# The semaphore wait in front of the first matmul block of a channel group, in a hybrid Conformer/SSD/MoE step

## The reference

```
u = xn @ w_in                                  # 1024 -> 10272 columns
glu_v, glu_g, z, xbc, dt_raw, gate_logit = split(u)
a    = causal_dwconv(glu_v * sigmoid(glu_g))   # 31 taps
xs, bm, cm = split(silu(causal_dwconv(xbc)))   # 4 taps
y, h = ssd(xs, dt, A, bm, cm, h0)              # chunked scan, and new states
y    = group_norm((y + d_skip * xs) * silu(z))
gates = sigmoid(gate_logit + gate_b)
```

## Time and profile before

| | us |
|---|---|
| median of 3 runs (1586.05 to 1589.49) | 1589.34 |
| the profiled execution | 1590.23 |
| its span, first to last instruction | 1588.5 |
| PE / DVE / ACT / POOL busy | 1383.0 / 1151.7 / 817.7 / 209.9 |

### The profile page before, as it was taken

The page is one execution under the profiler, slowest core; times in us unless marked ns, Lnnn a source line. Parts: engine busy times, 40 slices in busy tenths (PEclk is TensorE's granted clock), DMA queues, the critical chain, the costliest instruction groups (busy, mean ns, idle before and its releaser), DMA issues. The chain is left out here.

```text
span 1588.5 us, 25995 instructions
## 1 busy us (share of the span) xinstructions
PE 1383.0 (87%) x8618; PEld 1216.4 (77%) x8618; DVE 1151.7 (72%) x1626; ACT 817.7 (51%) x1437; POOL 209.9 (13%) x328
## 2 busy tenths in 40 slices
PE   4988998989989899898994899997449999999980
PEld 4887987979879798797982799985347878787860
DVE  4457796877968779687786454542739999999964
ACT  4343463534635346353452332422138999999961
POOL 1012030120301203012030000000200111111112
PEclk9888998989989899898995999999669999999995
DMA  6141623515235162351633825310678999999936
GB/s 191 41 127 55 167 72 93 157 54 169 67 97 152 54 169 67 101 148 54 173 90 129 247 63 171 117 54 19 273 257 310 371 371 372 370 374 374 373 117 238
DMA packets 191725, 273.99 MB, mean 172 GB/s; under 512 B 15661, under 2 KB 154117, under 8 KB 175252
## 3 DMA queue, kind: packets, MB, share of 16 engines
q1 hardware_dynamic: 179100, 248.36, 47.2%
q0 software_dynamic: 9536, 17.98, 3.2%
q10 hardware_dynamic: 3040, 7.03, 1.2%
HBM read 238.21 MB, written 52.48 MB: 183 GB/s over the span
## 5 line engine op out<-in xcount | busy, mean ns | idle before, releaser
L882 PE MATMUL pu<-xh,wh 128*128 128x304 f32 (+1 forms) x1280 | 297.2, 315 | 30.2 <-ACTq L720 28.6
L882 PE MATMUL pu<-xh,wl 128*128 128x304 f32 (+1 forms) x1280 | 282.2, 303 | 0.0
L882 PE MATMUL pu<-xl,wh 128*128 128x304 f32 (+1 forms) x1280 | 282.0, 303 | 0.0
L882 PEld LDWEIGHTS pu<-xh,wh 128*128 128x128 f32 x1280 | 208.7, 201 | 55.4 <-ACTq L720 30.6
L882 PEld LDWEIGHTS pu<-xl,wh 128*128 128x128 f32 x1280 | 210.4, 201 | 0.0
L882 PEld LDWEIGHTS pu<-xh,wl 128*128 128x128 f32 x1280 | 208.9, 200 | 0.0
L526 ACT ACTIVATE wh<-ring 128x1024 fp32r<-128x1024 f32 x80 | 84.4, 1055 | 226.8 <-PE pu L882 223.3
L1023 DVE SCALAR_TENSOR_TENSOR cacc<-a_p,gc,cacc 128x528 f32<-128x528 f32 x232 | 190.6, 822 | 5.0
L1742 DVE TENSOR_TENSOR W13l<-W,W13h 128x1024 fp32r<-128x1024 f32 x160 | 185.0, 1217 | 2.6 <-issue 0.3
L1726 ACT ACTIVATE W13h<-W 128x1024 fp32r<-128x1024 f32 x160 | 156.3, 1063 | 0.2 <-issue 0.2
L237 DVE TENSOR_TENSOR wl<-ring,wh 128x1024 fp32r<-128x1024 f32 x80 | 101.1, 1264 | 54.4 <-ACT wh L526 51.0
(11 more groups left out here) (396 smaller groups left out, 2633.6 us busy)
## 6 DMA issues: line engine op xcount, KB each, us to landing
W<-in_exp_w SPq DMA_DIRECT2D x100, 1024.0 KB, 7.4
ring<-in_w_in SPq DMA_DIRECT2D x80, 512.0 KB, 4.1
x<-in_exp_w SPq DMA_DIRECT2D x20, 1024.0 KB, 7.8
stage<-decay_rows SPq DMA_DIRECT2D x8, 1120.0 KB, 6.6
x<-in_state_ssm SPq DMA_DIRECT2D x16, 512.0 KB, 6.7
out_new_ssm_sample<-x SPq DMA_DIRECT2D x16, 512.0 KB, 5.7
wraw<-in_ssm_out_w SPq DMA_DIRECT2D x8, 1024.0 KB, 6.9
Ed<-decay_rows SPq DMA_DIRECT2D x32, 140.0 KB, 7.0
```

Source lines behind the costliest of these rows:

```text
L882: last = pe.matmul(u_cols(r, a, b), w[:, k % RING, j, :], x[:, j, a:b], start=(j == 0 and n == 0), stop=(j == KD - 1 and n == 2))
```

## The change

```
 def free(r):
 
-    pe.wait_ge(s_ufree, U0 + max(r, 1))
+    if r:
+        pe.wait_ge(s_ufree, U0 + r)
+    elif not is_first:
+        pe.wait_ge(s_ufree, U0)
 
 def block(k, first=0, end=KD):
```

## The result

The changed kernel takes 1538.45 us (median of 4 runs, 1536.58 to 1541.42) against 1587.69 us (4 runs, the three shown ahead among them, 1584.74 to 1589.49): a ratio of 0.9693, 95% interval 0.9668 to 0.9719, 49.2 us. The forecast was 1540 and a gain of 50.1. The profiled execution took 1536.82, its span is 1535.1 (1588.5 before).

The account below looks back on a forecast made before the run. PE was taken to bound the trunk, waiting for ScalarE at seven boundaries. These take 4 x 15.38 + 3 x 14.91 = 106.25, not 156.33: 1590.23 - 50.1 = 1540.1, given as 1540 us; range 1530 to 1563.

Parts of the forecast that it names:

- The releaser: At seven boundaries block 0 on PE waits for ScalarE's count, ended by block 9's tanh: 28.6 us together.
- the issuing side costs nothing: At block 0, PE's loop jump is hidden in the old idle time; a gap of 0.1 us was taken.
- The old idle time and the clock as two terms: At the boundaries, of 50.1 us gain, 28.6 is old idle time, the rest the clock less VectorE's new lateness.
- The first rival: At the boundaries only the idle time comes back and the clock stays down: 1561.6 us; chance 0.12.
- One slow stretch in four boundaries, none in three: Four boundaries keep one half-rate stretch of 3.42 us and take 15.38 us; three keep none and take 14.91.
- forecast sum of 106.25: Seven boundaries, block 9's end to block 1's start: 4 x 15.38 + 3 x 14.91, in place of 156.33 us.
- VectorE late next: At the boundaries VectorE's chain of state updates becomes late for PE's sums, but only by 0.9 us.
- by about 1 us: Sign expected in the changed kernel's profile: PE's sums at the boundaries wait this long for VectorE.
- forecast 14.91: Length in us of a boundary without a slow stretch, set by VectorE's chain of 13.07, then 0.05 and 1.79.
- The clock falling while the sums wait: With PE's sums waiting about 1 us, the clock could fall there; each further 3.42 us stretch costs 1.50.
- The slower rival: Clock falls at the sums and stays down in blocks 1 to 5: 13 us slower, 1603 us; chance 0.03.
- The rest of a group: Between boundaries the work starts from the same state as before and stays within 3 us of 76.5 us.

Follow-up runs that it names:

- The late read: Two extra tanh of block 9's tile on ScalarE ahead of the counting one: kernel before 1598.7 us, ratio 1.0061; changed kernel 1541.53 us, ratio 0.9708.
- The fill: Kernel before, old wait kept, 12 extra thrown-away matmuls in the idle time ahead of block 0: 1569.93 us, ratio 0.9899.
- the repeated change: The changed kernel run again unaltered, beside later edits: 1548.23 us (ratio 0.974), then 1541.49 us (ratio 0.9706).
- the two taps moved: Changed kernel with VectorE's two taps behind the last two state updates: 1540.32 us, ratio 0.9684; run again, 1536.49 us, ratio 0.9678.

## Why the prediction was right

**The releaser, and that the issuing side costs nothing.** Right: block 0 follows block 9 with no gap, so the loop's jump costs nothing that the profile shows. The late read shows the same from the other side: about 10 us in the kernel before, nothing clear of the intervals after.

**The old idle time and the clock as two terms.** Right. The fill gives the clock alone, 27.2 us of boundary in its profile and 18.8 us by the medians; the forecast had 28.6 for the idle time and the rest, some 21, for the clock less VectorE's lateness. The 28.6 and the 27.2 are more than the 48.8 of the boundaries; that VectorE's chain is late once the idle time is gone accounts for part of it, by argument and not by a run. The first rival, 1561.6 us, had the clock stay down: in four boundaries it did fall ahead of block 9's end, and came back 3.41 us later.

**One slow stretch in four boundaries, none in three.** Four and three it was, and the four stretches have the assumed length of 3.41. But they came earlier than assumed, at 233.92 for a block 9 that ends at 235.82, so less of them lies behind it: 14.72 to 15.22 us where 15.38 was forecast, with the loss moved ahead into the stretch before. The three that kept the clock were to be the fourth, fifth and sixth; they were the first, the sixth (up to the sums) and the seventh, so the count was right and the reason given for it was not. Which boundaries lose the clock differs between executions of the same program: six of seven fell in both profiles of the repeated change, four here. The count is luck; that the boundaries sum to 105 to 108 us in every profile of the change is not. The forecast sum of 106.25 against 107.51 holds three errors, two of them described next: 1.6 us too much for the four, 0.8 too little for two of the three, and 2.1 too little for the sixth. That the median came within 2 us of 1540 is partly luck too, as the same program gave 1548.23 on another occasion.

**VectorE late next.** Right as a mechanism, and the sums wait 1.6 us where the clock stays up, 0.34 where it falls; "by about 1 us" was between the two. The forecast 14.91 was 15.28 to 15.31, as VectorE is ready at 4.9 to 5.0 us behind block 9 there, not at 4.8, and stands still for 0.3 behind the samples' convolution. At the first boundary, where block 9 ends at 143.12 (VectorE, then PE):

```profile
146.90 1.23 DVE L237 TENSOR_TENSOR wl<-ring,wh 128x1024 fp32r<-128x1024 f32 x1
...
151.77 1.12 DVE L1026 SCALAR_TENSOR_TENSOR x<-x,Ed,pS 128x128 f32<-128x128 f32 x4 [0.29 <-DVE csum L1157]
```
```profile
156.62 1.21 PE L862 MATMUL pT<-th,ones 128*128 128x280 f32 x4 [1.61 <-DVE x L1026]
```

With the two taps moved no wait of the sums is longer than 0.34.

**The clock falling while the sums wait.** The slower rival named this place. It happened once of seven, with 1.7 us of cost and not more, which makes that boundary 17.04 us, outside the 14.9 to 15.4 that the prediction named:

```profile
616.25 2.23 PE L862 MATMUL pT<-th,ones 128*128 128x280 f32 x4 [1.61 <-DVE x L1026]
618.27 1.78 PE L862 MATMUL pS<-th,ones 128*128 128x280 f32 x4
```

The sums take 3.4 us there in place of 1.8; block 1 is at the full clock again from 619.62 on.

**The rest of a group.** 76.5 us forecast; 76.37 to 77.42 measured, 0.3 us more on average. Right within the bounds given.

## What to carry to other kernels

A wait on a count should name the tile that is written, not all reads so far; with two tiles in turn that is one count less. Work out the idle time behind such a wait as two prices, the time itself and the TensorE clock behind it: here the fill of the idle time gave back 18.8 us by the medians and 27.2 in its profile, beside 28.6 of idle time. Then look for what is ready just after the old release, since that is late next.

## What the runs showed that was not expected

Idle times of 1.27 to 2.82 us, ahead of matmuls of 32 rows, were followed by a fall of the clock at seven boundaries of seven, while with waits of 1.14 to 2.74 us ahead of a quarter it fell at one of seven. Behind such a fall the same quarters and additions ran at the half rate for 3.41, 6.83 or 17.07 us. With two extra instructions of 0.6 us on ScalarE the kernel before had runs that spread over 23 us (1587.32 to 1610.61; without them 4.6 us on that occasion, 11.8 us on another), and the change alone gave medians of 1538.45, 1548.23 and 1541.49 us on three occasions, the same program each time. What decides whether the clock falls, and when it comes back, in a given boundary stays open; no run here separates it.
